# Hybrid layer on one core: when POOL gates a scan chunk, and where the scan's small products stand

## The chip, the core and the metric

The kernel runs on one core of one Trainium2 chip. The metric is the device time of one execution in microseconds. The core has TensorE (PE in the profile; PEld is its weight load), VectorE (DVE), ScalarE (ACT), GpSimd (POOL) and SyncE (SP), which here only issues transfers.

## What is computed

One decoder layer on 512 tokens of width 1024: RMSNorm, one input projection, a Mamba-2 scan on 16 heads beside a forgetting attention on 16 heads, an output projection, and a mixture of 32 experts. The change touches the scan alone. Cut to what matters:

```
X = xs.reshape(b, nc, L, G, R, P)                  # L = 128 tokens a chunk, 4 chunks
cum = cumsum(dt * A, axis=2)
decay = exp(where(causal, cum_t[..., :, None] - cum_t[..., None, :], -inf))
CB = einsum('bclgn,bcsgn->bcgls', Cc, Bc)
y_diag = einsum('bcgls,bcgrls,bcsgrp->bclgrp', CB, decay, Xdt)
states = einsum('bclgn,bclgr,bclgrp->bcgrpn', Bc, exp(cum[:, :, -1:] - cum), Xdt)
h_in = scan(h -> exp(cum[:, :, -1]) * h + state, states)      # over the chunks
y_off = einsum('bclgn,bcgrpn,bclgr->bclgrp', Cc, h_in, exp(cum))
y = y_diag + y_off + X * d_skip
y_ssm = rmsnorm(y * silu(z))
```

## The kernel before, in words

The projections are cut into passes `n`. One pass is one PSUM bank (128 by 512) summed over eight tiles `k`; each tile is three fp32r matmuls (`three`, lines 1405 to 1407), since every operand is split into a high and a low part. Four passes share one block of eight weight slots. SP loads a slot into `raw`, ACT rounds it to `wh` (line 1022, `high`), and DVE or POOL takes the low part `wl = raw - wh` (line 282). SP may refill a slot of `raw` once the low part of the slot six earlier is made (line 398). `slots_after(n)` gives the slots whose high and low parts belong behind pass `n`: seven behind the third pass of a block, one behind the fourth.

The order of work on every engine is written out by hand, and semaphores join the engines. Each engine does its instructions strictly in its own program's order, so one that waits holds up all behind it.

The scan runs beside the sixteen q and k passes, i = 0 to 15 (n = 20 to 35), one chunk c to four passes. For chunk c:

- TensorE: `cb(c)` (C times B) before pass 4c+1, for chunk 0 inside pass 1; `y_off(c, 0)` after pass 4c+1; `diag(c, 0)` and `diag(c, 1)` inside pass 4c+2; after pass 4c+2 and the transposes of the one before, `y_off(c, 1)`, `diag(c, 2)` and `diag(c, 3)`; after pass 4c+3 `state(c, 0)` and `state(c, 1)`. After each pass come the transposes of the previous q or k tile (`qk_transpose`, line 1566).
- ACT: behind pass i a square (line 1120), Ln and Exp for its RMSNorm, the copy of the transposed tile, and then `cb_copy(c)`, `decays(c, 0)`, `decays(c, 1)` and, for c > 0, `decay_out_exp(c)` (line 1147) behind pass 4c; `decays(c, 2)` and `decays(c, 3)` behind pass 4c+1 (line 1141); then the highs.
- DVE: the sum of the squares (line 2064), the scaling (line 2070), M = decay * dt * CB (`m_product`, line 2083), `y_add(c, g)` (lines 2092, 2098, 2100), `state_keep(c, g)` (lines 2109 to 2117) and the lows, in the loop quoted below.
- POOL: `causal_decays(c)` masks the decay rows (line 775), `gate(c)` multiplies y by silu(z) (line 770), `scaled_x(c)` makes `Xs` for the states (line 763), `skip_term(c)` multiplies the conv output that was loaded into `y` by d_skip (line 755).
- SP: in a fixed order among the weight slots, `load_decay_rows(c)`, then for c >= 1 half a block later `load_conv_chunk(c)` (which overwrites `y`, so it waits for `gated`), `load_decay_out(c)`, and the next slots.

DVE's loop over the passes:

```
for i in range(16):
    qk_sum(i)
    qk_scale(i)
    ...
    if i % 4 == 1:
        m_product(c, 2)
        m_product(c, 3)
        y_add(c, 0)
    if i % 4 == 2:
        y_add(c, 1)
    if i % 4 == 3 and c < TC - 1:
        state_keep(c, 0)
        state_keep(c, 1)
    lows_after(N_QK + i)
```

Of the kernel before, what the change touches and what calls it, by code (L numbers as in the profile page):

```python
# [12 lines left out]
ALU = mybir.AluOpType  # L13
ACT = mybir.ActivationFunctionType
# [73 lines left out]
def hybrid_layer(nc, x, norm_mix_w, w_in, conv_w, conv_b, dt_bias, a_log, d_skip, ssm_norm_w, q_norm_w, k_norm_w,  # L88
# [10 lines left out]
    with ExitStack() as ctx:  # L99
# [422 lines left out]
        def _(sp):  # L522
# [52 lines left out]

            def load_decay_out(c):

                sp.wait_ge(sem("y_whole"), 2 * c)
                for odd in range(2):
                    sp.dma_start(decay_out[odd * HD:(odd + 1) * HD, :, :], decay_dram[c].rearrange("(q s) t -> s q t", s=2)[odd].partition_broadcast(HD))\  # L580
                        .then_inc(sem("decay_out_in"), 16)

            def load_first_bias():
                sp.wait_ge(sem("y_whole"), 2 * TC)
                for odd, name in ((0, "first_bias_even"), (1, "first_bias_odd")):
                    sp.dma_start(m[name][:], bias_dram[odd].partition_broadcast(P)).then_inc(sem("bias_in"), 16)

# [114 lines left out]
        def _(pool):  # L702
# [55 lines left out]
            def scaled_x(c):  # L758

                if c < TC - 1:  # L760
                    if c:
                        pool.wait_ge(sem("state_done"), 2 * c)
                    pool.tensor_tensor(heads(Xs[:]), heads(X[:, c, :]), over(dte[:, c, :], P, H, HD), ALU.mult)\
                        .then_inc(sem("x_to_end"), 1)

            def gate(c):

                pool.wait_ge(sem("y_whole"), 2 * c + 2)
                pool.wait_ge(sem("z_stored"), TC + c + 1)
                pool.tensor_tensor(zs[:, c, :], y[:], zs[:, c, :], ALU.mult).then_inc(sem("gated"), 1)  # L770

# [35 lines left out]
            for c in range(TC - 1):  # L807
                causal_decays(c + 1)
                gate(c)
                scaled_x(c + 1)  # L810
                skip_term(c + 1)
            gate(TC - 1)
            causal_bias(0)

# [192 lines left out]
        def _(act):  # L1007
# [147 lines left out]
            def y_square(c):  # L1155
# [2 lines left out]
                    act.wait_ge(sem("y_folded"), c)  # L1158
                act.activation(Pe[:, 0:2, :].rearrange("p a t -> p (a t)"), zs[:, c, :], ACT.Square).then_inc(sem("y_squared"), 1)

            act.preload_act_table_set("natural_log_exp_and_others")
            act.wait_ge(sem("steps_known"), 4)
            act.activation(dte[:], dte[:], ACT.Exp).then_inc(sem("dt_acts"), 1)
            act.activation(etot[:], tot[:, :, 0:H], ACT.Exp).then_inc(sem("dt_acts"), 1)
            for i in range(16):
                n = N_QK + i
                qk_square(i)
                qk_rstd(i)
                if i:
                    qk_store(i - 1)  # L1170

                if i % 4 == 0:
                    cb_copy(i // 4)
                    decays(i // 4, 0)
                    decays(i // 4, 1)
                    if i:
                        decay_out_exp(i // 4)
                if i % 4 == 1:
                    decays(i // 4, 2)
                    decays(i // 4, 3)  # L1180
                highs_after(n)
# [177 lines left out]
        def _(pe):  # L1359
# [209 lines left out]
            for i in range(17):  # L1569
                for k in range(KC):  # L1570
                    pass_tile(N_QK + i if i < 16 else N_V, k)
                    if i == 0 and k == 1:
                        x_transpose(NTR - 1)
                    if i == 1 and k == 1:
                        cb(0)
                    if i >= 2 and i % 4 == 2 and k in (1, 3):
                        diag(i // 4, k // 2)
                if i == 0:
                    continue
                qk_transpose(i - 1)  # L1580
                c, step = (i - 1) // 4, (i - 1) % 4
                if step == 0 and c:
                    y_off(c, 0)
                if step == 1:
                    if c:
                        y_off(c, 1)
                    diag(c, 2)
                    diag(c, 3)
                if step == 2 and c < TC - 1:
                    state(c, 0)  # L1590
                    state(c, 1)
                if step == 3 and c < TC - 1:
                    cb(c + 1)
# [304 lines left out]
        def _(dve):  # L1898
# [188 lines left out]
            def y_add(c, g):  # L2087
# [6 lines left out]
                if c:  # L2094
# [3 lines left out]
                    dve.tensor_tensor(yo, yo, ps[4][:], ALU.mult).then_inc(sem("y_off_scaled"), 1)  # L2098
                    dve.wait_ge(sem("y_off_scaled"), 2 * (c - 1) + g + 1)
                    dve.tensor_tensor(y[:, cols], y[:, cols], yo, ALU.add).then_inc(sem("y_whole"), 1)  # L2100
                else:
                    dve.tensor_copy(y[:, cols], y[:, cols]).then_inc(sem("y_whole"), 1)

            def state_keep(c, g):

# [14 lines left out]
            for i in range(16):  # L2120
                qk_sum(i)
                qk_scale(i)
                if i == 0:
                    dve.wait_ge(sem("dt_acts"), 5)
                    dve.tensor_tensor(dte[:], dte[:], sp[:, :, 0:H], ALU.mult).then_inc(sem("scales_known"), 1)
                    dve.wait_ge(sem("scales_known"), 1)
                c = i // 4
                if i % 4 == 0:
                    m_product(c, 0)
                    m_product(c, 1)  # L2130
                if i % 4 == 1:
                    m_product(c, 2)
                    m_product(c, 3)
# [352 lines left out]
```

## Time and profile before

| what | us |
|---|---|
| median of three runs | 722.3 (721.61 to 722.89) |
| the profiled execution | 722.08 |
| its span, first to last instruction | 720.3 |
| TensorE busy | 677.6 |
| DVE busy | 389.8 |
| ACT busy | 291.2 |
| POOL busy | 149.0 |

Times inside the profile count from the first instruction. The q and k passes with the scan lie between about 135 and 260 us. A row of the timeline gives the start, the duration, the engine, the line of the kernel and, in brackets, how long the engine was idle before and what released it. Several instructions of one kind in a row are put together in one row, with their number behind an x.

### The profile page before, as it was taken

What the parts mean: (1) busy time and instruction counts of PE and PEld (TensorE: products, weight loads), DVE (VectorE), ACT (ScalarE), POOL (GpSimd) and SP (SyncE); (2) the same over time, 40 slices, a digit from 0 to 9 for tenths busy, and PEclk for the clock granted to TensorE, in tenths of its full rate; (3) what the DMA queues carried; (4) which work ended last, traced back from release to release, by engine and by line L of the source; (5) the groups of instructions that cost most, each with busy time, mean ns of one, the idle gap of its engine ahead of it and who ended that gap; (6) DMA issues with size and microseconds to landing.
All of it is one profiled execution on the core that took longest, in us unless ns stands there. A gap on an engine that the chain in (4) does not pass through costs nothing.

```text
span 720.3 us, 10643 instructions
## 1 busy us (share of the span) xinstructions
PE 677.6 (94%) x3850; PEld 468.5 (65%) x3850; DVE 389.8 (54%) x834; ACT 291.2 (40%) x651; POOL 149.0 (21%) x178
## 2 busy tenths in 40 slices
PE   8999999999999999999999999979999978888975
PEld 7878888777777888766767788867434323333442
DVE  6866678878879665777787554471222211122211
ACT  5934534465655545665666423221212111121200
POOL 2300010114222110022342232020132321122331
PEclk9999999999999999999999999989999999999998
DMA  8333255426264343191030079689999999999993
GB/s 297 94 115 117 79 174 162 132 74 173 80 158 146 88 147 102 46 361 49 16 103 1 1 287 421 242 350 369 412 416 417 403 410 398 425 417 413 413 402 129
DMA packets 61160, 162.77 MB, mean 226 GB/s; under 512 B 14185, under 2 KB 25605, under 8 KB 49841
## 3 DMA queue, kind: packets, MB, share of 16 engines
q1 hardware_dynamic: 49120, 144.64, 53.7%
q0 software_dynamic: 6880, 9.02, 4.2%
q10 hardware_dynamic: 5104, 8.39, 3.1%
q8 instruction: 33, 0.54, 0.3%
q14 instruction: 23, 0.18, 0.1%
HBM read 157.67 MB, written 20.28 MB: 247 GB/s over the span
## 4 chain that ended last, share of the span: by engine, by line
PE 25%; SPq 14%; DMA 5%; DVE 2%; issue 2%; ACT 2%; POOL 0%; POOLq 0%; DVEq 0%; ACTq 0%
SPq L427 6%; PE bank L1816 5%; DMA s_gu<-in_w_expert_gate_dram 4%; SPq L475 4%; SPq L461 4%; PE bank L1845 3%; PE bank L1405 3%; PE bank L1407 3%; PE bank L1406 3%; PE bank L1787 2%; PE bank L1681 1%; PE bank L1638 1%; PE bank L1621 1%; PE bank L1763 1%; PE bank L1610 1%
## 5 line engine op out<-in xcount | busy, mean ns | idle before, releaser
L1816 PE MATMUL bank<-s_gu,s_xgT 128*64 128x512 f32 x352 | 84.4, 635 | 16.3 <-DMA s_gu<-in_w_expert_up_dram 16.3
L282 DVE TENSOR_TENSOR s_wl<-s_raw,s_wh 128x512 fp32r<-128x512 f32 x105 | 89.9, 903 | 12.3 <-ACT s_wh L1022 12.1
L1022 ACT ACTIVATE s_wh<-s_raw 128x512 fp32r<-128x512 f32 x120 | 72.7, 628 | 42.1 <-PE bank L1407 18.6
L1405 PE MATMUL bank<-s_wh,s_hTh 128*128 128x512 f32 x192 | 78.7, 410 | 0.0
L1407 PE MATMUL bank<-s_wh,s_hTl 128*128 128x512 f32 x192 | 75.1, 391 | 0.0
L1816 PEld LDWEIGHTS bank<-s_gu,s_xgT 128*64 128x64 f32 x352 | 28.8, 146 | 71.0 <-issue 71.0
L1406 PE MATMUL bank<-s_wl,s_hTh 128*128 128x512 f32 x192 | 74.9, 390 | 0.0
L1321 ACT ACTIVATE s_sg<-bank,s_slot_scale 128x256 f32<-128x256 f32 x16 | 7.6, 473 | 151.6 <-PE bank L1816 113.2
L1845 PE MATMUL bank<-s_dn,s_hidT 128*64 128x512 f32 x256 | 58.5, 598 | 1.6 <-DVE s_hidT L2388 1.6
L2388 DVE COPY s_hidT<-bank 128x256 f32<-128x256 f32 x16 | 6.8, 423 | 93.7 <-PE bank L1825 93.7
L2421 DVE SCALAR_TENSOR_TENSOR s_yrow<-bank,s_slot_scale,s_xg 128x512 f32<-128x512 f32 x30 | 21.2, 746 | 46.1 <-PE bank L1845 46.1
L898 POOL DMA_INDIRECT s_xg<-x_rows,s_slot_rows x16 | 16.6, 1038 | 140.5 <-DVE s_yrow L2421 105.4
L1405 PEld LDWEIGHTS bank<-s_wh,s_hTh 128*128 128x128 f32 x192 | 36.1, 188 | 10.1 <-issue 2.8
L1407 PEld LDWEIGHTS bank<-s_wh,s_hTl 128*128 128x128 f32 x192 | 36.0, 188 | 7.9
L1406 PEld LDWEIGHTS bank<-s_wl,s_hTh 128*128 128x128 f32 x192 | 36.1, 188 | 7.4 <-issue 0.7
L1405 PE MATMUL bank<-s_hTh,s_wh 128*128 128x512 f32 x96 | 39.2, 409 | 0.0
L1407 PE MATMUL bank<-s_hTh,s_wl 128*128 128x512 f32 x96 | 37.7, 392 | 0.0
L1406 PE MATMUL bank<-s_hTl,s_wh 128*128 128x512 f32 x96 | 37.4, 389 | 0.0
L1845 PEld LDWEIGHTS bank<-s_dn,s_hidT 128*64 128x64 f32 x256 | 17.0, 136 | 31.2 <-issue 27.1
L1193 ACT ACTIVATE s_Pe<-s_Pe,s_nmax 128x512 f32<-128x512 f32 (+3 forms) x41 | 22.6, 554 | 23.8 <-DVE s_nmax L2170 23.8
L282 POOL TENSOR_TENSOR s_wl<-s_raw,s_wh 128x512 fp32r<-128x512 f32 x15 | 22.3, 1490 | 41.8 <-ACT s_wh L1022 41.5
L775 POOL TENSOR_SCALAR_AFFINE_SELECT s_decay_rows<-s_decay_rows 128x2048 f32<-128x2048 f32 x4 | 8.6, 2160 | 107.5 <-DMA s_decay_rows<-decay_rows 107.5
(307 smaller groups left out, 1392.9 us busy)
## 6 DMA issues: line engine op xcount, KB each, us to landing
s_dn<-in_w_expert_down_dram SPq DMA_DIRECT2D x28, 1024.0 KB, 26.9
s_gu<-in_w_expert_gate_dram SPq DMA_DIRECT2D x26, 1024.0 KB, 28.0
s_gu<-in_w_expert_up_dram SPq DMA_DIRECT2D x24, 1024.0 KB, 28.0
s_raw<-in_w_in_dram SPq DMA_DIRECT2D x88, 256.0 KB, 4.1
s_raw<-in_w_out_dram SPq DMA_DIRECT2D x32, 256.0 KB, 3.5
s_gu<-in_w_expert_up_dram SPq DMA_DIRECT2D x12, 512.0 KB, 9.4
s_decay_rows<-decay_rows SPq DMA_DIRECT2D x4, 1024.0 KB, 4.7
s_gu<-in_w_expert_gate_dram SPq DMA_DIRECT2D x8, 512.0 KB, 8.8
```

The source lines that it names most:

```text
L282: eng.tensor_tensor(low, full, high.bitcast(F32), ALU.subtract).then_inc(sem(f"{what}_low_{low_engine(what, i)}"), 1)
L427: sp.dma_start(m[f"gu{b}"][:, half, which, :, :].rearrange("p k f -> p (k f)"), src).then_inc(sem(f"gu_in{b}"), 16)
L461: sp.dma_start(m[f"gu{p % NGU}"][:, half, which, rows, :], src).then_inc(sem(f"late_up_in{p}_{part}" if which else f"gu_in{p % NGU}"), 16)
L475: sp.dma_start(m[f"dn{b}"][:, half, :, :].rearrange("p k n -> p (k n)"), src).then_inc(sem(f"dn_in{b}"), 16)
L1022: act.activation(wh[:, i % HL, :], raw[:, i % RAW, :], ACT.Copy).then_inc(sem("w_high"), 1)
L1193: act.activation(p_tile(v), p_tile(v), ACT.Exp, bias=nmax[:, v:v + 1], scale=-1.0, accum_out=rsum[:, v:v + 1]).then_inc(sem("p_exp"), 1)
L1405: pe.matmul(dst, ah, bh, start=start, stop=False)
L1406: pe.matmul(dst, ah, bl, start=False, stop=False)
L1407: return pe.matmul(dst, al, bh, start=False, stop=stop)
L1816: last = pe.matmul(ps[j][r, :].rearrange("p (w f) -> p w f", w=2), m["xgT"][:, j, k, r], gu[:, half, :, k, :], start=(k == 0), stop=(k == ...
L1845: last = pe.matmul(ps[6 + nb][r, :], m["hidT"][:, j, at:at + CAP], dn[:, half, q, nb * BLK:(nb + 1) * BLK], start=(q == 0), stop=(q == 1))
L2421: dve.scalar_tensor_tensor(out=m["yrow"][:, j, cols], in0=ps[6 + nb][:], scalar=gates, in1=token_rows(p)[:, cols], op0=ALU.mult, op1=ALU.a ...
```

## The change

Seven edits:

- POOL: `gate(c)` waits, for c < 3, also for both parts of `state_keep(c)`. `scaled_x(c)` waits also until the four M products of its chunk are made, and stands behind `skip_term(c)`.
- DVE no longer copies y onto itself in chunk 0 to count `y_whole`; what waited for it waits for `y_diag` or for two counts fewer.
- SP: `load_decay_out(c)` waits for the sums of the chunk before (`y_diag` or `y_whole`) with the new counts; its place in the queue is the same.
- ACT: the square of pass 0 stands ahead of the table load; the exponentials for `dte` and `etot` stand behind the first two groups of decays of chunk 0.
- DVE: the product `dte * dt` stands behind the first two M products.
- TensorE: `cb(0)` two tiles later in pass 1; `diag(c, 0)` and `diag(c, 1)` one tile later in pass 4c+2.
- TensorE: `diag(c, 2)` and `diag(c, 3)` inside pass 4c+3, behind its tiles 1 and 3, in place of standing between the passes.

```diff
@@ -575,13 +575,16 @@
 
             def load_decay_out(c):
 
-                sp.wait_ge(sem("y_whole"), 2 * c)
+                if c == 1:
+                    sp.wait_ge(sem("y_diag"), 2)
+                else:
+                    sp.wait_ge(sem("y_whole"), 2 * (c - 1))
                 for odd in range(2):
                     sp.dma_start(decay_out[odd * HD:(odd + 1) * HD, :, :], decay_dram[c].rearrange("(q s) t -> s q t", s=2)[odd].partition_broadcast(HD))\
                         .then_inc(sem("decay_out_in"), 16)
 
             def load_first_bias():
-                sp.wait_ge(sem("y_whole"), 2 * TC)
+                sp.wait_ge(sem("y_whole"), 2 * (TC - 1))
                 for odd, name in ((0, "first_bias_even"), (1, "first_bias_odd")):
                     sp.dma_start(m[name][:], bias_dram[odd].partition_broadcast(P)).then_inc(sem("bias_in"), 16)
 
@@ -758,6 +761,7 @@
             def scaled_x(c):
 
                 if c < TC - 1:
+                    pool.wait_ge(sem("m_done"), 4 * c + 4)
                     if c:
                         pool.wait_ge(sem("state_done"), 2 * c)
                     pool.tensor_tensor(heads(Xs[:]), heads(X[:, c, :]), over(dte[:, c, :], P, H, HD), ALU.mult)\
@@ -765,7 +769,12 @@
 
             def gate(c):
 
-                pool.wait_ge(sem("y_whole"), 2 * c + 2)
+                if c:
+                    pool.wait_ge(sem("y_whole"), 2 * c)
+                else:
+                    pool.wait_ge(sem("y_diag"), 2)
+                if c < TC - 1:
+                    pool.wait_ge(sem("state_kept"), 2 * c + 2)
                 pool.wait_ge(sem("z_stored"), TC + c + 1)
                 pool.tensor_tensor(zs[:, c, :], y[:], zs[:, c, :], ALU.mult).then_inc(sem("gated"), 1)
 
@@ -807,8 +816,8 @@
             for c in range(TC - 1):
                 causal_decays(c + 1)
                 gate(c)
+                skip_term(c + 1)
                 scaled_x(c + 1)
-                skip_term(c + 1)
             gate(TC - 1)
             causal_bias(0)
 
@@ -1158,13 +1167,12 @@
                     act.wait_ge(sem("y_folded"), c)
                 act.activation(Pe[:, 0:2, :].rearrange("p a t -> p (a t)"), zs[:, c, :], ACT.Square).then_inc(sem("y_squared"), 1)
 
+            qk_square(0)
             act.preload_act_table_set("natural_log_exp_and_others")
-            act.wait_ge(sem("steps_known"), 4)
-            act.activation(dte[:], dte[:], ACT.Exp).then_inc(sem("dt_acts"), 1)
-            act.activation(etot[:], tot[:, :, 0:H], ACT.Exp).then_inc(sem("dt_acts"), 1)
             for i in range(16):
                 n = N_QK + i
-                qk_square(i)
+                if i:
+                    qk_square(i)
                 qk_rstd(i)
                 if i:
                     qk_store(i - 1)
@@ -1175,6 +1183,10 @@
                     decays(i // 4, 1)
                     if i:
                         decay_out_exp(i // 4)
+                    else:
+                        act.wait_ge(sem("steps_known"), 4)
+                        act.activation(dte[:], dte[:], ACT.Exp).then_inc(sem("dt_acts"), 1)
+                        act.activation(etot[:], tot[:, :, 0:H], ACT.Exp).then_inc(sem("dt_acts"), 1)
                 if i % 4 == 1:
                     decays(i // 4, 2)
                     decays(i // 4, 3)
@@ -1571,10 +1583,12 @@
                     pass_tile(N_QK + i if i < 16 else N_V, k)
                     if i == 0 and k == 1:
                         x_transpose(NTR - 1)
-                    if i == 1 and k == 1:
+                    if i == 1 and k == 3:
                         cb(0)
-                    if i >= 2 and i % 4 == 2 and k in (1, 3):
-                        diag(i // 4, k // 2)
+                    if i >= 2 and i % 4 == 2 and k in (2, 4):
+                        diag(i // 4, k // 2 - 1)
+                    if i >= 2 and i % 4 == 3 and k in (1, 3):
+                        diag(i // 4, 2 + k // 2)
                 if i == 0:
                     continue
                 qk_transpose(i - 1)
@@ -1584,8 +1598,6 @@
                 if step == 1:
                     if c:
                         y_off(c, 1)
-                    diag(c, 2)
-                    diag(c, 3)
                 if step == 2 and c < TC - 1:
                     state(c, 0)
                     state(c, 1)
@@ -2098,8 +2110,6 @@
                     dve.tensor_tensor(yo, yo, ps[4][:], ALU.mult).then_inc(sem("y_off_scaled"), 1)
                     dve.wait_ge(sem("y_off_scaled"), 2 * (c - 1) + g + 1)
                     dve.tensor_tensor(y[:, cols], y[:, cols], yo, ALU.add).then_inc(sem("y_whole"), 1)
-                else:
-                    dve.tensor_copy(y[:, cols], y[:, cols]).then_inc(sem("y_whole"), 1)
 
             def state_keep(c, g):
 
@@ -2120,14 +2130,14 @@
             for i in range(16):
                 qk_sum(i)
                 qk_scale(i)
-                if i == 0:
-                    dve.wait_ge(sem("dt_acts"), 5)
-                    dve.tensor_tensor(dte[:], dte[:], sp[:, :, 0:H], ALU.mult).then_inc(sem("scales_known"), 1)
-                    dve.wait_ge(sem("scales_known"), 1)
                 c = i // 4
                 if i % 4 == 0:
                     m_product(c, 0)
                     m_product(c, 1)
+                    if c == 0:
+                        dve.wait_ge(sem("dt_acts"), 5)
+                        dve.tensor_tensor(dte[:], dte[:], sp[:, :, 0:H], ALU.mult).then_inc(sem("scales_known"), 1)
+                        dve.wait_ge(sem("scales_known"), 1)
                 if i % 4 == 1:
                     m_product(c, 2)
                     m_product(c, 3)
```

## Rows read from the trace of the kernel before

**Rows 1.** Page, part 1: busy us, share of the span, instructions of each engine

```profile
PE 677.6 (94%) x3850; PEld 468.5 (65%) x3850; DVE 389.8 (54%) x834; ACT 291.2 (40%) x651; POOL 149.0 (21%) x178
```

**Rows 2.** TensorE's waits, 130 to 262 us: releaser, us in total, times, longest

```profile
PE bank L1534 <- ACT s_BC L1088: 0.8, 1, 0.8
PE bank L1566 <- DVE s_qn L2070: 0.8, 1, 0.8
PE bank L1524 <- DVE s_y L2092: 0.7, 1, 0.7
PE bank L1524 <- DVE s_M L2083: 0.6, 1, 0.6
```

**Rows 3.** Timeline of TensorE: start us, us, instruction, xcount, [idle before <-releaser]

```profile
220.06 1.16 PE L1546 MATMUL bank<-s_BC,s_Hst 128*128 128x128 f32 x8 [0.39 <-DVE s_decay_out L2098]
...
250.64 1.06 PE L1546 MATMUL bank<-s_BC,s_Hst 128*128 128x128 f32 x8
```

**Rows 4.** Timeline of TensorE around the small products of chunks 0 and 1

```profile
159.13 0.50 PE L1405 MATMUL bank<-s_wh,s_hTh 128*128 128x512 f32 x1
...
180.29 1.06 PE L1546 MATMUL bank<-s_BC,s_Hst 128*128 128x128 f32 x8
181.10 0.48 PE L1405 MATMUL bank<-s_wh,s_hTh 128*128 128x512 f32 x1
...
182.34 0.40 PE L1407 MATMUL bank<-s_wh,s_hTl 128*128 128x512 f32 x1
...
183.26 0.50 PE L1405 MATMUL bank<-s_wh,s_hTh 128*128 128x512 f32 x1
...
188.75 1.06 PE L1546 MATMUL bank<-s_BC,s_Hst 128*128 128x128 f32 x8
...
190.76 0.50 PE L1405 MATMUL bank<-s_wh,s_hTh 128*128 128x512 f32 x1
```

**Rows 5.** Timeline of DVE in chunks 0 and 2

```profile
161.29 9.99 DVE L282 TENSOR_TENSOR s_wl<-s_raw,s_wh 128x512 fp32r<-128x512 f32 x7
...
174.53 0.69 DVE L282 TENSOR_TENSOR s_wl<-s_raw,s_wh 128x512 fp32r<-128x512 f32 x1
175.14 0.68 DVE L2064 TENSOR_REDUCE s_qss<-s_sq 128x8 f32<-128x512 f32 x1
...
222.54 0.68 DVE L2092 TENSOR_TENSOR s_y<-s_y,bank 128x512 f32<-128x512 f32 x1
...
224.77 6.50 DVE L282 TENSOR_TENSOR s_wl<-s_raw,s_wh 128x512 fp32r<-128x512 f32 x7
...
235.24 0.69 DVE L2115 TENSOR_TENSOR s_Hst<-s_Hst,bank 128x512 f32<-128x512 f32 x1
```

**Rows 6.** Timeline of POOL in chunk 0 and at the start of chunk 1

```profile
163.21 2.81 POOL L770 TENSOR_TENSOR s_zs<-s_y,s_zs 128x1024 f32<-128x1024 f32 x1
...
175.92 1.90 POOL L755 TENSOR_TENSOR s_y<-s_y,s_dskip_of 128x1024 f32<-128x1024 f32 x1 [6.39 <-DMA s_y<-conv_rows]
```

**Rows 7.** Timeline of ACT in chunks 2 and 3

```profile
211.87 1.05 ACT L1147 ACTIVATE s_decay_out<-s_decay_out 128x1024 f32<-128x1024 f32 x1
212.81 0.58 ACT L1120 ACTIVATE s_sq<-bank 128x512 f32<-128x512 f32 x1
...
240.81 1.06 ACT L1147 ACTIVATE s_decay_out<-s_decay_out 128x1024 f32<-128x1024 f32 x1
```

**Rows 8.** Timeline of the SP queue, loads for chunk 1

```profile
168.23 0.38 SPq L574 DMA_DIRECT2D s_y<-conv_rows  x1
168.65 1.67 SPq L580 DMA_DIRECT2D s_decay_out<-decay_rows  x2
```

**Rows 9.** View of the tile decay_out, its six loads

```profile
DMA to landing us min/median/max: 6.4/6.8/9.2
```

**Rows 10.** Windows at a stop of TensorE: length, busy (PE, PEld, DVE, ACT, POOL), clock, DMA

```profile
582.00:587.00 5.00, 0.01 (x2) 0.03 (x1) 1.41 (x2) 0.00 (x0) 2.04 (x2) 1.00 1.03 384
587.00:590.40 3.40, 3.40 (x8) 1.10 (x10) 0.00 (x0) 0.00 (x0) 1.58 (x1) 0.50 1.02 422
```

## The prediction, made before the change was run

> **What bounds the kernel now.** I read the page first. TensorE is busy 94% of the span [rows 1]. So up to about 480 us time is lost or won only where TensorE stands still or is given more to issue; after that the expert weights bound it, and their loads start when TensorE's passes free the buffers, so a delay before 480 us is passed on whole. Next I read TensorE's waits in the stretch of the q and k passes, where everything that the change touches lies [rows 2]. There are few: 0.8 us before the first `cb`, 0.6 and 0.7 us before products of chunk 0, 0.8 us before the transposes of pass 3; a fifth, 0.4 us, stands in the timeline before `y_off(2, 1)` at 220.06 [rows 3]. Against start-to-start times without a wait these are 0.9, 0.7, 0.8, 0.9 and 0.6 us: 3.9 us is all that can be won here. Then I read what runs beside the passes on DVE, POOL, ACT and SP, because the change mostly moves waits there.
>
> I number the sixteen passes i = 0 to 15; chunk c has i = 4c to 4c+3. The marker of a chunk is the start of `y_off(c, 1)` on TensorE, after pass 4c+2: 188.75, 220.06 and 250.64 us for c = 1, 2, 3 [rows 3, 4].
>
> **The products spread.** In a chunk, `diag(c, 2)` and `diag(c, 3)` go from one cluster between passes into the next pass. A `diag` inside a pass: from the matmul at 182.34 to the next of the pass at 183.26 is 0.92 us where 0.23 is normal (the five steps from 181.10 to 182.34 are 1.24 us, the first some 0.1 longer), and the first matmul behind it again takes 0.1 longer, so 0.8 us each. The cluster: 188.75 to 190.76 holds `y_off` and both, 2.01 us, and `y_off` alone is 180.29 to 181.10, 0.81; so 1.2 us for both [rows 4]. Spread costs 1.6 - 1.2 = 0.4 us a chunk, 1.6 in all, on the path, nothing to hide it. Shifting `cb(0)` and the first two `diag` by a tile or two costs nothing and covers about 0.9 us of their waits.
>
> **First square ahead of the table load; two exponentials later.** The square, its sum and the rstd chain start earlier by the table load that stood ahead of them, the decays of chunk 0 with them, and POOL's first `scaled_x` no longer runs beside the M products. The waits before `cb(0)` and `diag(0, 0)` go. The wait behind the cluster (0.8 us with the y_add it waits for) goes with the cluster's move. If the square brought a second table load of its own, these 1.6 us would stay lost; that is in the range.
>
> **Two copies of y dropped.** `tensor_copy` of y is 0.43 us twice on DVE, beside passes: nothing on the path.
>
> **DVE freed from POOL.** In chunk 0 the seven low parts take 9.99 us [rows 5], while one alone takes 0.60 to the next instruction (174.53 to 175.14), so 4.2 us for seven; the rest lies under POOL's causal select, gate and scaled X, of which the gate took 2.81 us from 163.21 [rows 6]. The Trainium skill ("SBUF — State Buffer", section "SBUF: two separate sides") has it that a VectorE instruction with two SBUF inputs and a GpSimd instruction that reads SBUF exclude each other for the whole instruction. By that rule alone the change would take some 5 us off VectorE in chunk 0 and be a gain; it says nothing of who waits for the delayed GpSimd work. The trace agrees with the rule. In the sum: the wait before the transposes of pass 3 goes. Pass 3 itself begins 3.7 us earlier than its 159.13 us [rows 4] (0.9 + 0.7 + the cluster's 1.2 and 0.8), at 155.4.
>
> **The new wait: what is queued behind the gate.** This decides. `gate(c)` now waits for both parts of `state_keep(c)`, which DVE does at the end of the chunk. Behind it on SP stand, in order, `load_conv_chunk(c+1)` (waits for `gated`), the two `load_decay_out(c+1)` and the weight slots. The earlier semaphore that `load_decay_out` gets helps nothing, since SP has not come past the conv load. Then on ACT `decay_out_exp(c+1)` stands in program order before the square of pass 4c+5, and behind that square come rstd, the last eight decay exponentials, M, y_add and `y_off(c+1, 1)`, for which TensorE waits.
>
> The prices. Chunk 2: the y_add of its second half began at 222.54, the seven lows took 6.50 us, the state was kept at 235.24 + 0.69 = 235.93: 13.4 us from one to the other [rows 5]. ACT took `decay_out` at 240.81, only 4.9 us after the state was kept [rows 7]. From now on between these two lie: the gate, between 1.90 us (POOL's multiply of the same size at 175.92, beside no low part) and 2.81 us (as it is) [rows 6], I take 2.4, since DVE has one low part there only; SP's conv issue and the two issues behind it, the last one begun some 1.5 us after the first (168.23, then 168.65 with 1.67 for the pair) [rows 8]; and the landing of the last issue, 6.4 to 9.2 us, median 6.8 over the six [rows 9]. I take 8.1, above the median: the second of a pair has the conv load and the first ahead of it, and the weight slots are issued right behind it as before. Together 2.4 + 0.1 + 1.5 + 8.1 = 12.1 us where 4.9 are free.
>
> The cycle from marker to marker then is: `y_off` 0.8, four tiles of 0.69 and two `diag` of 0.8 before the second y_add may start, 5.2 us; 13.4 less the 2.3 us of lows no longer blocked, plus 0.4 for the seventh low, whose raw slot is loaded only after the first low: 16.7 us when the state is kept; plus 12.1 is 28.8; the exponential to the square behind it 0.94 (211.87 to 212.81), and from there to `y_off` 7.25 (212.81 to 220.06, where DVE's product ended the wait) [rows 3, 7]. Sum 37.0 us. Before, the cycles were 31.3 and 30.6 [rows 3, 4]. So +5.7 for chunk 2 and +6.4 for chunk 3.
>
> Chunk 1's marker, from chunk 0: pass 3 at 155.4, its second `diag` done 4.4 later, y_add 0.7, lows 4.2 and 0.9 for POOL's select and the seventh raw: 165.6. From the end of the lows to the kept state were 3.3 us before (171.2 to 174.5), so 168.9. Plus 12.1, 0.94 and 7.25: 189.2, 0.5 us later than 188.75. All that chunk 0 wins is given back here; TensorE alone would have been there at about 185.7.
>
> After the last marker the spread adds 0.4. Sum without the clock: 0.5 + 5.7 + 6.4 + 0.4 = 13.0 us.
>
> **The clock.** TensorE then stands still before three markers, some 3.5, 6 and 6 us. The only such stops in this trace are in the expert stage: after 5 us without work the granted clock was 0.50, 1.2 GHz, from 587.0 to 590.4, and 8 matmuls ran in that time [rows 10]. Half of 3.4 us, 1.7 us, is lost each time, and it lies in the cycle, since y_add waits for those very passes. Three times 1.7 is 5.1; nothing of it if the clock stays. The stop of 5 us is the nearest row, so I take it whole. Sum: 13.0 + 5.1 = 18.1 us.
>
> **Rivals.** *The loads are not late* (ends faster). TensorE's own cycle would be 31.0 us, the unblocked 30.6 and 0.4 for the spread. It is the bound again if gate, issues and landing together end within 12.1 - (37.0 - 31.0) = 6.1 us of the kept state. Then the first marker comes at 185.7, 3.0 us early, the cycles give -0.3 and +0.4 and the last spread 0.4: 2.5 us faster, 719.8. For it speaks that the conv and decay_out loads find an idle DMA queue; against it that no issue of decay_out landed under 6.4 us, and the gate comes on top. *Late but cheap*: landings of 6.4 us and no lower clock: cycles of 35.3 us, the first marker at 187.5, so -1.2 + 4.0 + 4.7 + 0.4 = 7.9 us slower, 730. *Won and lost alike*: landings of about 3 us, half of the shortest row: cycles of 31.9 us, marker 1 at 185.7: -3.0 + 0.6 + 1.3 + 0.4 = -0.7 us, no change to be seen, 721.6.
>
> The Trainium skill ("DMA: Bandwidth & Descriptors", section "Anatomy of one DMA") puts a transfer's fixed part at about 2 us, and at its 436 GB/s the 1 MB would take 2.4 more, an estimate from that page of 4.4 us from the first issue; it would make the last rival come true. The trace disagrees: from the first conv issue on, this load took twice that.
>
> **How the numbers follow.** The profiled execution took 722.08 us, its span 720.3, and the median is 722.3, so both serve. Forecast: 722.3 + 18.1 = 740.4. Its own bounds: landings of 6.4 or 9.2 and gates of 1.9 or 2.8 move each of three cycles by -2.2 or +1.5, so -6.6 or +4.5; the clock takes 0 to 5.1. That gives 728.7 to 744.9; with a longer half-speed stretch or the second table load, 747. Chances: late loads as forecast 0.72, late but cheap 0.15, loads not late 0.08, won and lost alike 0.05. Range 727 to 747. A measurement of this kernel tells 0.2%, 1.4 us, from no change: faster 0.08, same 0.05, slower 0.87.
>
> **What would show it.** In the profile after: `decay_out_exp` on ACT with idle time ended by the decay_out load, three times; the gates 16 to 17 us behind the markers; `y_off(c, 1)` with the longest waits of TensorE, on the DVE product of decay_out; cycles of about 37 to 39 us; the granted clock at half behind these waits. No wait at the first `cb` nor at the first `diag`; the lows of chunk 0 in 4 to 5 us. It is wrong if ACT reaches the exponentials after they have landed, above all if the state is kept much earlier than 16.7 us behind the marker.

## The result, and the profile after

The changed kernel takes 735.56 us (median of 5 runs, 735.14 to 736.38) against 722.37 (5 runs, 721.61 to 723.36): ratio 1.0174, 95% interval 1.0156 to 1.0192, so 13.2 us slower. The direction and the range of the prediction held; its 18.1 us were 5 too many. The experiments then showed that one part which the prediction had priced at 1.6 us, the spread, costs 4.0 us or more.

The page after, part 1 (busy us, share of the span, instructions), beside [rows 1]:

```profile
span 734.3 us, 10647 instructions
PE 685.8 (93%) x3850; PEld 471.2 (64%) x3850; DVE 377.2 (51%) x832; ACT 290.6 (40%) x651; POOL 147.4 (20%) x178
```

The span grew by 14.0 us, with the same TensorE instructions. TensorE's waits from 130 to 275 us (in total, times, longest), where [rows 2] had four small ones:

```profile
PE bank L1558 <- DVE s_decay_out L2110: 9.2, 3, 3.9
PE bank L1417 <- DVE s_wl L282: 0.2, 1, 0.2
```

The waits before the first `cb` and the first `diag` are gone. In their place stand three stops before the markers, `y_off(c, 1)`, on VectorE's product with `decay_out`. The timeline of TensorE at the three markers, beside [rows 3, 4]:

```profile
187.22 1.16 PE L1558 MATMUL bank<-s_BC,s_Hst 128*128 128x128 f32 x8 [1.68 <-DVE s_decay_out L2110]
...
221.94 2.07 PE L1558 MATMUL bank<-s_BC,s_Hst 128*128 128x128 f32 x8 [3.56 <-DVE s_decay_out L2110]
...
260.09 2.08 PE L1558 MATMUL bank<-s_BC,s_Hst 128*128 128x128 f32 x8 [3.93 <-DVE s_decay_out L2110]
```

The markers stand at 187.22, 221.94 and 260.09 us. Before they stood at 188.75, 220.06 and 250.64. The cycles between them are 34.7 and 38.2 us, where they were 31.3 and 30.6. The first marker comes 1.5 us earlier, and 9.5 us have been lost by the third. The rest comes behind it (below).

The chain that makes a marker late is read backwards. First the timeline of ACT, beside [rows 7]: each exponential of `decay_out` stands behind idle time that the load ended.

```profile
178.92 1.06 ACT L1156 ACTIVATE s_decay_out<-s_decay_out 128x1024 f32<-128x1024 f32 x1 [3.52 <-DMA s_decay_out<-decay_rows]
...
213.75 1.06 ACT L1156 ACTIVATE s_decay_out<-s_decay_out 128x1024 f32<-128x1024 f32 x1 [4.64 <-DMA s_decay_out<-decay_rows]
214.71 0.58 ACT L1129 ACTIVATE s_sq<-bank 128x512 f32<-128x512 f32 x1
...
251.89 1.06 ACT L1156 ACTIVATE s_decay_out<-s_decay_out 128x1024 f32<-128x1024 f32 x1 [5.35 <-DMA s_decay_out<-decay_rows]
```

Then the queue that issued that load (SP), the gate on POOL that SP waited for, and the kept state on DVE that the gate waited for, in the same cycle; beside [rows 8, 6, 5]:

```profile
207.09 0.38 SPq L574 DMA_DIRECT2D s_y<-conv_rows  x1
207.51 1.27 SPq L583 DMA_DIRECT2D s_decay_out<-decay_rows  x2
```

```profile
204.16 2.85 POOL L779 TENSOR_TENSOR s_zs<-s_y,s_zs 128x1024 f32<-128x1024 f32 x1 [12.59 <-issue]
```

```profile
203.34 0.69 DVE L2125 TENSOR_TENSOR s_Hst<-s_Hst,bank 128x512 f32<-128x512 f32 x1
```

The state was kept at 203.34 + 0.69 = 204.03, the gate ran to 207.01, SP issued from 207.09 to 208.78, and ACT began at 213.75. That is 9.7 us from kept state to exponential, where the prediction had 12.1. The difference is the landing. The view of the tile `decay_out`, beside [rows 9]:

```profile
DMA to landing us min/median/max: 5.0/5.5/6.2
```

Windows on the clock (columns as in [rows 10]):

```profile
214.00:221.30 7.30, 4.38 (x26) 3.08 (x24) 4.35 (x12) 5.10 (x14) 0.65 (x1) 1.00 0.37 124
221.30:228.10 6.80, 6.16 (x23) 4.75 (x24) 3.05 (x4) 2.26 (x5) 3.26 (x2) 0.50 0.28 117
228.10:258.80 30.70, 27.98 (x146) 21.22 (x144) 18.31 (x38) 14.70 (x37) 4.75 (x2) 1.00 0.37 103
258.80:265.70 6.90, 5.61 (x22) 4.25 (x22) 3.18 (x5) 2.25 (x5) 0.00 (x0) 0.51 0.00 0
```

Twice in these passes TensorE ran at half its clock, 1.2 GHz, for 6.8 and 6.9 us. Both stretches began during a stop and lasted some 6 us beyond its end. No fall followed the first stop.

Behind the last marker, TensorE at the transposes of pass 15:

```profile
278.50 0.66 PE L1578 MATMUL bank<-s_ident,s_qn 128*128 128x128 f32 x4 [1.21 <-DVE s_qn L2082]
```

These transposes are the last scan-side point that can be compared. Before they began at 264.18, 13.5 us behind the marker, now 18.4 us behind it. Sum: -1.5 (first marker), +3.4 and +7.6 (cycles), +4.9 (behind the last marker), 14.3 us, against 14.0 in the span.

### The profile page after: what moved, and what is told of

It reads as the page before. It is cut to its first block and busy times, and to the rows that moved or that the text cites. A ratio compares the mean times of both kernels' runs of the same rounds, so it can differ in the third digit from the quotient of the medians.

```text
span 734.3 us, 10647 instructions
## 1 busy us (share of the span) xinstructions
PE 685.8 (93%) x3850; PEld 471.2 (64%) x3850; DVE 377.2 (51%) x832; ACT 290.6 (40%) x651; POOL 147.4 (20%) x178
## 5 line engine op out<-in xcount | busy, mean ns | idle before, releaser
L282 DVE TENSOR_TENSOR s_wl<-s_raw,s_wh 128x512 fp32r<-128x512 f32 x105 | 78.0, 788 | 13.1 <-ACT s_wh L1031 12.7
L1417 PE MATMUL bank<-s_wh,s_hTh 128*128 128x512 f32 x192 | 80.9, 421 | 0.2 <-DVE s_wl L282 0.2
L2054 DVE SCALAR_TENSOR_TENSOR s_acc<-s_up,s_cvec,s_acc 128x512 f32<-128x512 f32 x36 | 28.7, 797 | 1.3
```

The lines of the kernel that those rows point to most:

```text
L282: eng.tensor_tensor(low, full, high.bitcast(F32), ALU.subtract).then_inc(sem(f"{what}_low_{low_engine(what, i)}"), 1)
L1417: pe.matmul(dst, ah, bh, start=start, stop=False)
L2054: ins = dve.scalar_tensor_tensor(out=a, in0=up[:, f % 2, t:t + T], scalar=tap[t], in1=a, op0=ALU.mult, op1=ALU.add)
```

## The experiments

I measured twelve kernels in three groups, each beside the kernel before on the same chip: 722.90 for e1, e2, e3 and e5, 722.68 for e4, e6, e7 and e8, 722.67 for e9 to e12. The points of TensorE's timeline that the text uses are gathered here. The last column is the time from the last marker to the transposes of pass 15.

| kernel | median us | over before | ratio, 95% interval | marker 1 | cycle 2 | cycle 3 | to the end |
|---|---|---|---|---|---|---|---|
| before | 722.4 |  | 1 | 188.75 | 31.31 | 30.58 | 13.54 |
| change | 735.6 | +13.2 | 1.0156 to 1.0192 | 187.22 | 34.72 | 38.15 | 18.41 |
| e1 no gate wait | 724.1 | +1.2 | 1.0003 to 1.0033 | 185.12 | 32.16 | 33.27 | 15.85 |
| e2 gate wait alone | 729.7 | +6.8 | 1.0056 to 1.0123 | 189.89 | 33.82 | 33.91 | 13.60 |
| e3 decay_out first | 722.3 | -0.6 | 0.9984 to 1.0014 | 184.81 | 31.10 | 31.08 | 15.86 |
| e4 spread alone | 729.2 | +6.5 | 1.0076 to 1.0106 | 188.41 | 35.48 | 32.19 | 15.85 |
| e5 group back | 727.5 | +4.6 | 1.0044 to 1.0085 | 186.41 | 32.99 | 33.62 | 13.64 |
| e6 = e3 and e5 | 718.1 | -4.6 | 0.9938 to 0.9964 | 185.54 | 30.47 | 30.48 | 13.53 |
| e7 = e1 and e5 | 718.2 | -4.5 | 0.9931 to 0.9955 | 185.25 | 30.47 | 30.48 | 13.54 |
| e8 head alone | 720.9 | -1.7 | 0.9968 to 0.9988 | 187.57 | 31.24 | 30.61 | 13.53 |
| e9 = e4, lows first | 726.9 | +4.3 | 1.0036 to 1.0074 | 190.85 | 32.96 | 32.26 | 14.08 |
| e10 = e3, lows first | 720.3 | -2.4 | 0.9953 to 0.9980 | 185.28 | 31.06 | 31.07 | 14.07 |
| e11 = e8, POOL's part | 718.8 | -3.9 | 0.9919 to 0.9962 | 185.94 | 30.47 | 30.48 | 13.53 |
| e12 = change, lows first | 729.4 | +6.7 | 1.0056 to 1.0107 | 186.74 | 33.39 | 34.68 | 16.63 |

The points are those of one execution, and that one need not be near the median. Of e5 the profiled execution (723.9 us) was one of its two quickest; its ten runs went from 723.6 to 729.7. Those of e3 (720.4) and e6 (717.2) were the quickest of theirs, those of e4 (730.3) and e9 (729.2) the slowest. From the transposes of pass 15 to the end of the span it was 455.4 (e6) to 458.0 us (e10), with 456.1 before and 455.8 after, so a difference of a microsecond or two between two medians need not lie in the scan.

### Is it the gate's wait, and through which queue?

**e1**, the change without the gate's wait:

```
-                if c < TC - 1:
-                    pool.wait_ge(sem("state_kept"), 2 * c + 2)
```

> The changed kernel without the gate's wait for the kept state; all else as changed. Before is 722.4 us, changed is 735.6. Theory A (the late gate holds back the loads of the next chunk, and ACT waits for decay_out): the ACT waits for decay_out (3.5, 4.6 and 5.3 us) go. The gate then lies beside the low parts again and blocks them for about 2.3 us, behind a second y_add that the spread has made about 3 us later, so the kept state is late for cb by some 1.4 us a chunk: about 724 to 727. Rival B (the small products spread into passes are themselves what costs): stays at 732 or more. Rival C (only the stops of TensorE's clock matter, not the waits): no clear figure, but no stop, no clock loss: 727 to 730.

**e2**, the kernel before with the gate's wait and nothing else:

```
                 pool.wait_ge(sem("y_whole"), 2 * c + 2)
+                if c < TC - 1:
+                    pool.wait_ge(sem("state_kept"), 2 * c + 2)
```

> The kernel before with one line more: the gate waits for the kept state. Theory A, with the landing of 5.6 us that the changed kernel shows: marker 1 about 1.5 us late, cycles of 33.1 and 31.3 us for 31.3 and 30.6, no fall of the clock: 725 to 728, so only a third of the loss, since the second y_add is still early. If the gate's wait by itself were the whole loss: 733 to 736. Rival B: 722 to 723.

**e3**, the change with its gate wait, and SP's two loads in the other order:

```
-                    load_conv_chunk(i // KC - 6)
                     load_decay_out(i // KC - 6)
+                    load_conv_chunk(i // KC - 6)
```

> The changed kernel with the two lines of SP swapped: decay_out of the next chunk is loaded ahead of the conv chunk, so it does not stand behind the gate. The gate stays late. Theory A: ACT finds decay_out landed, the conv chunk lands about 6.8 us behind the gate, early enough for the skip term: 720 to 723. If the late gate hurts by something other than decay_out (POOL's skip term late, contention, weight slots held back): 728 or more. Rival B: 732 or more.

e1 took 724.1, at the lower edge of what my theory gave: of 13.2 us over before 1.2 are left, so the wait costs 12.0. e2 took 729.7, 1.7 above its band: alone the wait costs 6.8 us. Its cycle 3 was 33.9 us where 31.3 was expected, and in its cycle 2 the clock fell, which theory A had excluded. e3 took 722.3 with the wait kept. The waits of ACT on that load are these, of the changed kernel and then of e2; e3 has none:

```profile
ACT s_decay_out L1156 <- DMA s_decay_out<-decay_rows: 13.5, 3, 5.3
```

```profile
ACT s_decay_out L1149 <- DMA s_decay_out<-decay_rows: 12.5, 3, 5.2
```

In e3 the gate still runs late. The timelines of SP and then of POOL in e3:

```profile
163.12 1.35 SPq L583 DMA_DIRECT2D s_decay_out<-decay_rows  x2
171.25 0.38 SPq L574 DMA_DIRECT2D s_y<-conv_rows  x1
```

```profile
168.34 2.83 POOL L779 TENSOR_TENSOR s_zs<-s_y,s_zs 128x1024 f32<-128x1024 f32 x1 [7.96 <-issue]
```

The two `decay_out` issues go out 5.2 us ahead of the gate, and the conv load alone waits for it. So a gate that waits for the kept state costs nothing. What costs is that `load_decay_out` stands behind it on SP. That settles the first question.

### What does the spread cost?

**e5**, the change with `diag(c, 2)`, `diag(c, 3)` in one group behind `y_off(c, 1)` and the first two back on tiles 1 and 3:

```
-                    if i >= 2 and i % 4 == 2 and k in (2, 4):
-                        diag(i // 4, k // 2 - 1)
-                    if i >= 2 and i % 4 == 3 and k in (1, 3):
-                        diag(i // 4, 2 + k // 2)
+                    if i >= 2 and i % 4 == 2 and k in (1, 3):
+                        diag(i // 4, k // 2)
...
                         y_off(c, 1)
+                    diag(c, 2)
+                    diag(c, 3)
```

> The changed kernel with diag(c, 2) and diag(c, 3) back between the passes and the first two after tiles 1 and 3; the late gate stays. Theory A+ (the loop gate, load, exponential, M, y_off, second y_add, lows, kept state sets the cycle, and the spread lengthens it by the 3 us by which the second y_add comes later): cycles of about 32 us, no fall of the clock: 721 to 725. Theory A without that term (the late gate alone costs, the spread only its 0.4 us a chunk): 732 to 734. Rival B: 720 to 722.

It took 727.5, 4.6 us over before instead of 13.2, and 2.5 above my band. So the spread is worth 8.6 us in the change. I did it alone and undid it in the two kernels without a late load.

**e4**, the kernel before with TensorE's new order only (the edit of e5 the other way round, and `cb(0)` at tile 3); **e6** is e3 with the edit of e5, **e7** is e1 with it:

> The kernel before with one part of the change: TensorE's order, diag(c,0), (c,1) moved one tile later, diag(c,2), (c,3) spread into the pass ahead of step 1, cb(0) at tile 3. POOL, SP, ACT and DVE keep their old orders, so no gate waits for a state. Theory A (my prediction's price for this part, 0.4 us a chunk beside hidden waits): 723.5 to 725. Theory C (the spread itself lengthens the cycle, since e5 with the cluster put back came 8 us below the change): 727 to 731, with new waits of TensorE near the cluster's old place. If it is 722 to 725, the spread costs only where decay_out is late already, and e5's saving is an interaction.

> The changed kernel with two things undone: SP loads decay_out ahead of the conv chunk that waits for the gate (as in e3), and diag(c,2), (c,3) are back in one group behind y_off(c,1) (as in e5). Theory A: the loss is decay_out behind the gate, so this is at or a little below e3: 719 to 723. If the spread costs its own 0.4 us a chunk, it is 1 to 2 us below e3. If it is above 724, the group has a cost of its own in the new order.

> The changed kernel without the gate's wait for the kept state (as in e1) and with diag(c,2), (c,3) back in one group behind y_off(c,1) (as in e5). Left of the change are the dropped copies, the square ahead of the table load, scaled_x behind the decays, SP's earlier bounds. Theory A: 720 to 724, no more than 2 us below e1. If it is below 719, those remaining parts gain something that the prediction put at nothing.

The spread alone costs 6.5 us (729.2), where the prediction had 1.6 and theory C 4 to 8. Undone, it gives 4.0 us back to e3 (e6, 718.1) and 5.7 to e1 (e7, 718.2). Both end below my bands, and to drop the gate's wait (e7) or to let it hold up nothing (e6) comes to the same time. Where the time goes is seen on TensorE and on DVE in e4 (waits from 130 to 300 us, and DVE's from 150 to 300; in total, times, longest):

```profile
PE bank L1566 <- DVE s_qn L2070: 4.2, 4, 1.3
PE bank L1534 <- DVE s_Hst L2115: 1.3, 2, 0.7
```

```profile
DVE s_y L2092 <- PE bank L1524: 9.0, 4, 2.8
```

The last of these rows has none like it before. In VectorE's program the second `y_add` of a chunk comes ahead of the seven weight lows, and it needs `diag(c, 3)`, which TensorE now does four tiles into the next pass. The timeline of DVE in chunk 1 of e4:

```profile
193.76 0.69 DVE L2092 TENSOR_TENSOR s_y<-s_y,bank 128x512 f32<-128x512 f32 x1 [2.78 <-PE bank L1524]
...
195.81 8.16 DVE L282 TENSOR_TENSOR s_wl<-s_raw,s_wh 128x512 fp32r<-128x512 f32 x7
203.90 0.68 DVE L2064 TENSOR_REDUCE s_qss<-s_sq 128x8 f32<-128x512 f32 x1
205.18 0.69 DVE L2070 TENSOR_TENSOR s_qn<-bank,s_qr 128x512 f32<-128x512 f32 x1 [0.61 <-ACT s_qr L1015]
```

VectorE stands idle for 2.78 us. The lows, the square's sum and the scaled q behind them come late, and TensorE waits for that q before the transposes:

```profile
205.93 0.66 PE L1566 MATMUL bank<-s_ident,s_qn 128*128 128x128 f32 x4 [1.30 <-DVE s_qn L2070]
207.25 1.15 PE L1534 MATMUL bank<-s_BC 128*128 128x128 f32 x4 [0.66 <-DVE s_Hst L2115]
```

**e9**, **e10**, **e12** test that: e4, e3 and the change with three of the seven lows ahead of that `y_add`:

```
                 if i % 4 == 2:
+                    lows_after(N_QK + i, 0, 3)
                     y_add(c, 1)
+                    lows_after(N_QK + i, 3)
...
-                lows_after(N_QK + i)
+                if i % 4 != 2:
+                    lows_after(N_QK + i)
```

> e4 (the kernel before with the spread alone, 729.2) with one more edit: VectorE makes the first three of the seven weight lows ahead of its second y_add of a chunk, not behind it. Theory D: the spread costs so much because that y_add stands in VectorE's program behind the last diag, which now ends 2.8 us after VectorE is free, and the lows, the square's sum and the scaled q behind it come late for TensorE's transposes (four waits of 1.2 us). Then 723 to 726. Rival C2: the two diag inside a pass and the slower first tiles behind them cost it on TensorE itself: 728 to 730, as e4.

> e3 (the change with decay_out loaded first, 722.3) with the same edit of VectorE's order: the whole spread kept, nothing late on SP. Theory D: it comes down to 718.5 to 721, within 2 us of e6 (718.1), where the group of diag was put back instead. Rival C2: 721.5 to 723.5, as e3.

> The changed kernel (735.6) with the same edit of VectorE's order alone; the gate still waits for the kept state and decay_out still stands behind it. Theory A with D: the kept state comes by up to 2.8 us earlier in each cycle, and what hangs on it in line with it, so 726 to 731, near e5 (727.5). Rival C2: 734 to 737.

VectorE's wait for `diag(c, 3)` is gone in all three. e9 comes down by 2.3 us to 726.9, above my band; e10 by 1.8 to 720.3 (in the table the gain stands behind the last marker, 14.07 for 15.86); e12 by 6.5 to 729.4, both as the theory had it. In e10 the view of TensorE's waits from 130 to 275 us is empty, so what e10 keeps above e6 is the spread's own price on TensorE. By the table that is 0.6 us in each cycle and 0.5 behind the last marker, less 0.3 at the first: 1.5 of the 2.2 us between e10 and e6; the other 0.7 is less than what the profiled executions differ by behind the scan. So the idle time on VectorE makes up nearly half of the 4.0 us that the spread costs where nothing else is late. e9 keeps two waits at the transposes, 2.2 us together, one of 1.5 before a `cb` and one of 0.9 before its last marker. In its profiled execution, the slowest of its eight, the clock fell to half too, behind a wait of 1.54 us; whether it fell in the others is not shown. The windows of e9 around it:

```profile
170.00:174.00 4.00, 2.26 (x10) 1.24 (x9) 3.39 (x5) 1.45 (x4) 1.34 (x2) 1.00 1.04 235
174.00:177.50 3.50, 3.50 (x13) 3.09 (x13) 2.82 (x5) 1.64 (x6) 1.29 (x1) 0.51 1.00 268
```

and in e4, behind the two waits shown above:

```profile
204.00:207.30 3.30, 1.34 (x8) 0.66 (x6) 2.62 (x5) 2.09 (x5) 0.00 (x0) 1.00 0.94 275
207.30:210.60 3.30, 3.30 (x10) 2.82 (x11) 2.62 (x5) 0.57 (x3) 1.54 (x1) 0.51 1.15 233
```

That accounts for e4's cycle of 35.5 us: 1.3 and 0.7 of waits, 1.7 at half the clock (an estimate, half of 3.3), 0.6 of issue, on 31.3.

The same runs show how the two losses add. The load of `decay_out` behind the gate costs 9.2 us where the group is kept (e6 to e5), 9.1 with the spread and three lows first (e10 to e12), and 13.8 with the spread in the order of the change (e3 to the change). So some 4.6 us of the change's loss come from the two together: the late `y_add` holds the lows, the kept state stands behind them, and the gate behind that. What the clock costs is in these figures and was not taken out: in the profiled executions it fell twice in the change, once in e12 and not at all in e5.

### Which part gains?

**e8**, the kernel before with the head alone: first square ahead of the table load, the two exponentials and DVE's product of them behind the first decays.

```
+            qk_square(0)
             act.preload_act_table_set("natural_log_exp_and_others")
-            act.wait_ge(sem("steps_known"), 4)
-            act.activation(dte[:], dte[:], ACT.Exp).then_inc(sem("dt_acts"), 1)
-            act.activation(etot[:], tot[:, :, 0:H], ACT.Exp).then_inc(sem("dt_acts"), 1)
```

> The kernel before with one part of the change: ScalarE's first square ahead of the table load, its exponentials of the steps behind the first decays, and VectorE's product of them behind the first two products with the mask. Theory A: at most 0.6 us gained or lost in the start of the scan, and the rest follows its own chain: 721.5 to 723.5, no difference that can be measured. Rival: an earlier first marker is kept through all four chunks: 720 to 721.5.

**e11**, e8 with POOL's part but for the gate's wait:

```
                 if c < TC - 1:
+                    pool.wait_ge(sem("m_done"), 4 * c + 4)
...
                 gate(c)
-                scaled_x(c + 1)
                 skip_term(c + 1)
+                scaled_x(c + 1)
```

> e8 (the kernel before with the new head, 720.9) with POOL's part of the change: scaled_x waits for the chunk's four products with the mask and stands behind the next chunk's skip term. Left out are the copies of y, SP's new bounds, the gate's wait and the spread. e7, with the dropped copies and SP's bounds too, took 718.2. Theory: what e7 gained comes from VectorE being less blocked by POOL, so this is 718 to 719.5. Rival: it comes from the dropped copies, which let chunk 0's end and the loads behind y_whole come earlier: 720.5 to 721.5.

e8 takes 1.7 us off. That is the rival, not my theory: the first marker comes 1.2 us earlier, and the cycles (31.24 and 30.61) keep it. e11 takes off 3.9, inside my band, and its time is that of e6 and e7 (718.1, 718.2), which also drop the copies and move SP's bounds; these two edits show no gain of their own. What POOL's order does is seen in the seven lows of chunk 0 on DVE: 9.99 us before [rows 5], 8.18 in e8, 6.48 in e11, and 4.27 + 0.69 in the change, where POOL's gate is away from them as well. The timelines of DVE, of e8, of e11 and of the change:

```profile
161.91 8.18 DVE L282 TENSOR_TENSOR s_wl<-s_raw,s_wh 128x512 fp32r<-128x512 f32 x7
```

```profile
161.07 6.48 DVE L282 TENSOR_TENSOR s_wl<-s_raw,s_wh 128x512 fp32r<-128x512 f32 x7
```

```profile
160.51 4.27 DVE L282 TENSOR_TENSOR s_wl<-s_raw,s_wh 128x512 fp32r<-128x512 f32 x6
165.13 0.69 DVE L282 TENSOR_TENSOR s_wl<-s_raw,s_wh 128x512 fp32r<-128x512 f32 x1 [0.36 <-ACT s_wh L1031]
```

The Trainium skill ("SBUF — State Buffer", section "SBUF: two separate sides") says that a VectorE instruction with two SBUF inputs and a GpSimd one that reads SBUF take turns; these three rows agree. It would have called the change a gain, and for VectorE it is one. The time was decided on SP.

e6, e7 and e11 beat both kernels, by 0.5 to 0.6% below the kernel before.

## Why the prediction was right, and where it was not

**The new wait** held link by link. The state of chunk 0 was kept at 169.05 (168.9 foreseen), that of chunk 1 16.8 us behind the marker (16.7), and that of chunk 2, at 241.56, 19.6 us behind it, with the stretch at half the clock in between. From the exponential to the marker it was 8.2 to 8.3 us in all three cycles (0.94 + 7.25). TensorE's waits are on the DVE product of `decay_out`, and none stands at the first `cb`. e1, e2 and e3 show the cause by experiment: the loads behind the gate on SP, not the gate itself.

**The landing** was mis-sized. I took 8.1 us for the last issue "above the median"; it landed after 5.7 (173.24 to 178.90) and 5.6. With the gate at 2.85 (2.4 foreseen) and the last issue begun 1.15 after the first (1.5), the 12.1 us became 9.9, 9.7 and 10.3, so 6.4 us less over three chunks. I had read the landings of before as a property of the load. They were that of a queue with other loads in it. The DMA view of before, 196 to 212 us, has seven weight slots beside these loads, and that of the change, 204 to 216 us, has four:

```profile
s_raw<-in_w_in_dram SPq DMA_DIRECT2D x7, 256.0 KB, 4.7
s_y<-conv_rows SPq DMA_DIRECT2D x1, 512.0 KB, 6.9
s_decay_out<-decay_rows SPq DMA_DIRECT2D x2, 256.0 KB, 7.9
```

```profile
s_raw<-in_w_in_dram SPq DMA_DIRECT2D x4, 256.0 KB, 5.6
s_y<-conv_rows SPq DMA_DIRECT2D x1, 512.0 KB, 4.3
s_decay_out<-decay_rows SPq DMA_DIRECT2D x2, 256.0 KB, 5.3
```

Before, four slots were issued from 193.79 us on and were in flight when the conv load went out at 198.24. After, the four ahead were issued at 195.34, the conv load at 207.09. I had the idle queue among the arguments for a rival and did not put it into the price. In e1, where the issues are as early as before, the median is 7.0 us; in e3, where they are apart from the conv load, 5.2. The Trainium skill ("DMA: Bandwidth & Descriptors", section "Anatomy of one DMA") has about 2 us and the bytes at 436 GB/s for one transfer issued by GpSimd, and from it came the estimate of 4.4 us for all three from the first issue on. Here SP issues them, which the prediction did not say. Measured are 6.8 (172.09 to 178.90), so the estimate is nearer than my 9.6 and still too short. The landings of 5.0 to 6.2 us were also shorter than the 6.4 of the rival "late but cheap" and of my lower bound. So that rival's 730 was too low not for the load, but for the clock and the spread.

**The clock** was foreseen as three falls of 1.7 us. It fell twice, for twice as long, and not after the first stop. The state of chunk 2 was kept 2.8 us later behind its marker than that of chunk 1, and the end is 2.6 us longer than in e3, which has the same order: 5.4 us in place of 5.1. That these sums agree is luck. I took the 3.4 us from a row of 8 matmuls in the expert stage. The trace of before also has a stretch of twice that length, which I did not use. It lies in the router, among small products, behind waits of no more than 0.91 us:

```profile
477.80:484.60 6.80, 4.73 (x32) 4.43 (x31) 5.61 (x28) 1.80 (x4) 1.99 (x3) 0.50 0.82 342
```

**The spread** is the step that failed in its mechanism. "Spread costs 0.4 us a chunk" counted TensorE's issue only; that part measures 0.6 (e10 beside e6). I saw that the second `y_add` starts later and counted it inside the late cycle (5.2 us from the marker). I did not see that it holds the seven lows where nothing else is late, nor what it does behind the last marker, where I wrote "the spread adds 0.4": the end grew by 2.3 us in e1, e3 and e4 alike. Alone it costs 6.5 us (e4), without late loads 4.0 to 5.7, in the change 8.6.

**The sum by its own steps**: 18.1, less 6.4 for the landing and what goes with it, plus 0.3 for the clock, plus 1.9 for the end (2.3 for 0.4), is 13.9; links of 0.1 or 0.2 make up the rest to the profile's own 14.3. So the forecast was within 5 us partly because the errors of the landing and of the spread had opposite signs, and because the clock's two errors cancelled.

**The rival "loads not late"** had the right condition and the wrong price. e3 is that case, and took 722.3, not 719.8: the first marker came earlier than foreseen (184.81 for 185.7) and the cycles were 31.1 (31.0), but the end cost 2.3 us for 0.4. By these points it is 1.3 us faster than before, by the medians 0.6, where the rival had 2.5. e11, with no spread, has the first marker at 185.94 and cycles of 30.5: "the unblocked 30.6".

**The head** and **DVE freed from POOL** were put as won and given back. e8 and e11 measure what they win: 1.7 us, and 2.2 more. **The copies** were put at nothing, and nothing of theirs is seen.

Open: how the loss divides where the wait alone costs 6.8 us (e2), 9.1 in the new order without the spread (e7 to e5) and 12.0 beside it (e1 to the change). The late `y_add` is a shown part of that. The clock is an argued part (5.4 us in the profiled change, one short fall in e2, none in the profiled e5) and was not taken away by itself. Open too is what decides whether the clock falls (below).

## What to carry to other kernels

A wait is paid for by what stands behind it in its queue, not by the instruction that waits: the same gate wait cost nothing once the urgent load was issued ahead of it, so look at the queue's order before removing a wait. When a product moves later on TensorE, move its consumer in the other engine's program too: an in-order engine that waits for it holds all its unrelated work, and the price shows far from the edit, here at the transposes. Take a transfer's duration from a row with the same traffic around it; if a change moves its issue, ask what will still be in flight then.

## What the hardware showed that I had not expected

**When the clock falls.** Stops of much the same length went both ways. Half the clock followed stops of 3.56 and 3.93 us in the change and one of 3.49 in e12, each for about 6.8 us. None followed the longest stop of e2, 3.17 us before its last marker, nor the two of 2.25 and 2.88 in e5. But shorter falls of 3.3 us came behind a wait of 2.06 us in e2, 1.54 in e9 and 1.30 with 0.66 in e4. The windows of e2, its short fall and then its longest stop:

```profile
187.00:191.30 4.30, 2.24 (x20) 1.78 (x20) 4.06 (x10) 1.05 (x4) 0.00 (x0) 1.00 0.66 244
191.30:194.60 3.30, 3.30 (x21) 2.58 (x16) 2.54 (x4) 1.27 (x4) 2.01 (x1) 0.51 0.03 5
255.00:262.00 7.00, 4.38 (x34) 3.71 (x35) 6.22 (x13) 2.71 (x7) 0.00 (x0) 1.00 0.00 0
```

The length of a stop alone did not tell it in these runs, nor in the router before (above), where no wait ahead of the fall was longer than 0.91 us and one of 1.31 began with it. A wait of 1.5 us (e9) was followed by a fall that costs some 1.7 more, an estimate from half of its 3.5 us, and one of 3.2 us (e2) by none.

**The gate** took 2.83 to 2.85 us late, beside one weight low, one sum and one scaled q of VectorE, as much as the 2.81 early amid the lows [rows 6]. I had expected less there (2.4), between that row and the 1.90 us of a POOL multiply [rows 6]. But the second operand of that multiply is repeated along the row (`dskip_of`, broadcast), the gate's is a full tile: it is not the same work. So being moved away from the lows did not shorten the gate.
